# The opening of a two-layer attention and expert kernel written as one block

## The reference, cut to what matters

```python
def adaln_params(cvec, w, b):
    m = jax.nn.silu(cvec) @ w + b
    return [mi[..., None, :] for mi in jnp.split(m, ADA_CHUNKS, axis=-1)]

def modulate(x, g, shift, scale):
    return rmsnorm(x, g) * (1 + scale) + shift

        h = modulate(x, norm1_g[i], sh1, sc1)
        hc = modulate(xc, norm1_g[i], csh1, csc1)
```

## Time and profile before

| what | value |
|---|---|
| runs before, us | 4536.93, 4542.0, 4542.59 |
| median of the runs | 4542.0 us |
| span of the profiled execution | 4538.3 us |
| busy: PE / PEld / DVE / ACT / POOL | 80% / 58% / 49% / 35% / 4% |
| DMA, mean over the span | 200 GB/s, 909.64 MB |
| mean granted TensorE clock | 0.887 of full speed |

### The profile page before, as it was taken

One profiled execution on the slowest core, in us unless ns is written; L12 is line 12 of the kernel. 1 busy time (PEld: TensorE's weight loads), 2 busy tenths in 40 slices (PEclk: granted clock), 3 DMA queues, 4 the chain that ended last, 5 costly groups with the idle time before them and its releaser, 6 DMA issues. The chain is left out here.

```text
span 4538.3 us, 58330 instructions
## 1 busy us (share of the span) xinstructions
PE 3652.0 (80%) x19637; PEld 2640.8 (58%) x19637; DVE 2230.0 (49%) x4378; ACT 1566.0 (35%) x2639; POOL 168.9 (4%) x344
## 2 busy tenths in 40 slices
PE   5977977968699999998796689998368667777776
PEld 3747965447588888886565579997236322222223
DVE  3634643899566666665358778884441100000001
ACT  3433432128444444443241666663121111011111
POOL 0006610000000000000000000000000000000000
PEclk8988988979899999999897899999659788788878
DMA  4230021516644454443201499994212499999996
GB/s 161 73 132 13 13 96 52 210 45 199 217 175 182 185 185 175 168 173 126 98 20 65 126 362 312 312 312 140 116 38 84 189 428 427 427 427 428 427 428 273
DMA packets 331813, 909.64 MB, mean 200 GB/s; under 512 B 46592, under 2 KB 167168, under 8 KB 306176
## 3 DMA queue, kind: packets, MB, share of 16 engines
q1 hardware_dynamic: 331648, 907.42, 52.9%
HBM read 854.38 MB, written 52.95 MB: 200 GB/s over the span
## 5 line engine op out<-in xcount | busy, mean ns | idle before, releaser
L1929 PE MATMUL pd<-h_parts,u_parts 128*128 128x512 f32 x2048 | 471.3, 390 | 37.5 <-DVE u_parts L2015 37.5
L1942 PE MATMUL po<-act_parts,v_parts 128*128 128x512 f32 x2048 | 483.6, 393 | 10.3 <-DVE v_parts L2020 3.7
L1929 PEld LDWEIGHTS pd<-h_parts,u_parts 128*128 128x128 f32 x2048 | 385.6, 188 | 118.1 <-DVE u_parts L2015 37.7
L1942 PEld LDWEIGHTS po<-act_parts,v_parts 128*128 128x128 f32 x2048 | 383.6, 189 | 105.4 <-DVE v_parts L2020 22.4
L3053 PE MATMUL pb<-moe_ring,moe_xs 128*32 128x512 f32 x2048 | 334.4, 759 | 137.1 <-DMA moe_ring<-in_moe_gu 119.3
L3104 DVE TENSOR_TENSOR moe_hidden<-moe_silu,pg 128x512 f32<-128x512 f32 x16 | 11.0, 688 | 659.6 <-PE pg L3042 533.1
L2133 PE MATMUL pd<-h_parts,u_parts 128*128 128x256 f32 x2048 | 268.2, 284 | 38.6 <-DVE u_parts L2212 38.6
L2133 PEld LDWEIGHTS pd<-h_parts,u_parts 128*128 128x128 f32 x2048 | 264.6, 192 | 50.3 <-DVE u_parts L2212 39.2
L2143 PE MATMUL po<-v_parts,act_parts 128*128 128x512 f32 x1024 | 260.0, 398 | 0.9 <-DVE act_parts L2228 0.9
L395 PE MATMUL ps<-h_terms,w_terms 128*128 128x512 f32 x960 | 225.1, 398 | 40.6 <-DVE w_terms L408 40.6
L3069 PE MATMUL pd<-moe_ring,moe_hidden 128*32 128x512 f32 x1024 | 167.4, 790 | 100.6 <-DMA moe_ring<-in_moe_down 87.9
(11 more groups left out here) (472 smaller groups left out, 5846.8 us busy)
## 6 DMA issues: line engine op xcount, KB each, us to landing
moe_ring<-in_moe_gu SPq DMA_DIRECT2D x128, 2048.0 KB, 26.3
u_stream<-in_peer_u SPq DMA_DIRECT2D x256, 512.0 KB, 6.0
v_stream<-in_peer_v SPq DMA_DIRECT2D x256, 512.0 KB, 4.3
moe_ring<-in_moe_down SPq DMA_DIRECT2D x64, 2048.0 KB, 26.2
ada_ring<-in_ada_w SPq DMA_DIRECT2D x24, 2048.0 KB, 13.4
g_stream<-peer_gates SPq DMA_DIRECT2D x128, 256.0 KB, 5.9
peer_gates<-gate_stage_even SPq DMA_DIRECT2D x3, 8192.0 KB, 30.3
peer_gates<-gate_stage_odd SPq DMA_DIRECT2D x3, 8192.0 KB, 30.3
```

Source lines behind the costliest of these rows:

```text
L1929: m = pe.matmul(pd[:, j, 0:T], us[:, j, w, c], h[:, w, c], start=(c + w == 0), stop=(c == DC - 1 and w == 1))
L1942: m = pe.matmul(po[:, (c + b) % 4, 0:T], vs[:, j, w, (c + b) * P:(c + b) * P + P], aparts[:, 4 * half + j, w], start=(j + w == 0), stop=(j ...
```

## The change

`opening` takes the place of the first `load`, of `ada_params`, of the `load` of `deltas` and of `modulated` for layer 0. It is one block. SP issues `params`, `xT`, `consts`, the four modulation fetches, the two `w_qkv` fetches and `w_ab`, and `deltas`, one behind the other, and at the end waits for `deltas`. ACT does silu as soon as `params` is there and `c_silu` is cleared, then the squares when `xT` is there, the root, the four copies of the modulation, the shifts. PE does the sums first and then the modulation. DVE does eps, reciprocal, `place` (the addition of the bias), `mod_mult` and the 16 products, each of the first ones waiting for the one before through `Chain`. The ring's four slots are no longer a tile of their own: three are stretches of `qkvT` (8 chunks each) and one is `oT`. The silu and clear of `AdaParams` become methods, with their two blocks kept for the instances without a given ring; the `fetch` argument goes. The semaphores of the ring get names that the expert stream uses too.

```diff
--- before.py
+++ after.py
@@ -542,37 +542,40 @@
 
     TURN = 4
...
-    def __init__(self, k, ctx, layer, ada_w, params, consts, mod, fetch=True, first=0, groups=6 * D // BANK):
+    def __init__(self, k, ctx, layer, ada_w, params, consts, mod, first=0, groups=6 * D // BANK, ring=None):
-        self.slot = [k.sig(f"ada_slot{n}") for n in range(self.TURN)]
+        self.slot = [k.sig(f"ring_slot{n}") for n in range(self.TURN)]
-        self.ring = k.sb(ctx, "ada_ring", [self.TURN, DC, BANK])
+        if ring is None:
+            own = k.sb(ctx, "ada_ring", [self.TURN, DC, BANK])
+        self.ring = ring or [own[:, n] for n in range(self.TURN)]
-        with nc.Block() as block:
-            if fetch:
-                @block.sync
-                def _(sp):
-                    for g in range(self.TURN):
-                        self.fetch(sp, g)
-
-            @block.vector
-            def _(dve):
-                dve.memset(self.cs[:], 0.0)
-        with nc.Block() as block:
-            @block.scalar
-            def _(act):
-                act.activation(self.cs[:, :, 0:2], PARAMS(params, "cc").rearrange("p (c v) -> p c v", v=2), ACT.Silu)
+        if ring is None:
+            with nc.Block() as block:
+                @block.vector
+                def _(dve):
+                    self.clear(dve)
+            with nc.Block() as block:
+                @block.scalar
+                def _(act):
+                    self.squash(act)
+
+    def clear(self, dve):
+        return dve.memset(self.cs[:], 0.0)
+
+    def squash(self, act):
+        return act.activation(self.cs[:, :, 0:2], PARAMS(self.params, "cc").rearrange("p (c v) -> p c v", v=2), ACT.Silu)
-        sp.dma_start(self.ring[:, g % self.TURN], self.src[:, :, at:at + BANK]).then_inc(self.slot[g % self.TURN].h, DMA_DONE)
+        sp.dma_start(self.ring[g % self.TURN], self.src[:, :, at:at + BANK]).then_inc(self.slot[g % self.TURN].h, DMA_DONE)
...
@@ -607,43 +610,113 @@
...
+    def place(self, dve):
+        j0, n = 4 * self.first, 4 * self.GROUPS
+        a0 = PARAMS.at["ada_b"][0] + 48 * self.layer + j0
+        bias = self.params[:, a0:a0 + n].rearrange("p (j v) -> p j v", v=1).broadcast_to([P, n, 2])
+        return dve.tensor_tensor(self.mod[:, j0:j0 + n], self.pt[:, 0, 0:2 * n].rearrange("p (j v) -> p j v", v=2), bias, ALU.add)
+
+    def done(self):
+        for s in self.slot:
+            s.done(DMA_DONE * (self.GROUPS // self.TURN))
+        for s in (self.used, self.part_ready, self.turned):
+            s.done(self.GROUPS)
+
     def finish(self, k):
         with k.nc.Block() as block:
             @block.vector
             def _(dve):
-                j0, n = 4 * self.first, 4 * self.GROUPS
-                a0 = PARAMS.at["ada_b"][0] + 48 * self.layer + j0
-                bias = self.params[:, a0:a0 + n].rearrange("p (j v) -> p j v", v=1).broadcast_to([P, n, 2])
-                dve.tensor_tensor(self.mod[:, j0:j0 + n], self.pt[:, 0, 0:2 * n].rearrange("p (j v) -> p j v", v=2), bias, ALU.add)
-        for s in self.slot:
-            s.done(DMA_DONE * (self.GROUPS // self.TURN))
-        for s in (self.used, self.part_ready, self.turned):
-            s.done(self.GROUPS)
-
-
-def ada_params(k, layer, ada_w, params, consts, mod):
-
+                self.place(dve)
+        self.done()
+
+
+def opening(k, xT, hT, params, consts, deltas, mod, W, ring, begin):
+
+
+    nc = k.nc
+    one = CONSTS(consts, "one")
+    got_params, got_consts, got_x, got_deltas = (k.sig(x) for x in ("open_params", "open_consts", "open_x", "stage_loaded"))
+    sq, summed, rooted, chain, scaled = (k.sig(x) for x in ("nrm_sq", "nrm_sum", "nrm_root", "dve_chain", "nrm_scaled"))
+    spans = ((0, 0, CTX), (1, CTX, TALL))
+    CLEAR, RSTD, MOD, MULT = 1, 3, 4, 5
     with ExitStack() as ctx:
-        ada = AdaParams(k, ctx, layer, ada_w, params, consts, mod, groups=4)
-        with k.nc.Block() as block:
+        ada = AdaParams(k, ctx, 0, W["ada_w0"], params, consts, mod, groups=4, ring=ring)
+        mult = k.sb(ctx, "mod_mult", [2, DC])
+        x2 = k.sb(ctx, "x_squared", [DC, TALL])
+        rstd = k.sb(ctx, "rstd", [TALL])
+        ps = k.banks(ctx, 1)
+        with nc.Block() as block:
             @block.sync
             def _(sp):
-                ada.sync(sp)
+                sp.dma_start(params[:], W["params"]).then_inc(got_params.h, DMA_DONE)
+                sp.dma_start(xT[:], W["xT"]).then_inc(got_x.h, DMA_DONE)
+                sp.dma_start(consts[:], W["consts"]).then_inc(got_consts.h, DMA_DONE)
+                ada.begin(sp)
+                for x in begin:
+                    x.begin(sp)
+                sp.dma_start(deltas[:], W["deltas"]).then_inc(got_deltas.h, DMA_DONE)
+                sp.wait_ge(got_deltas.h, got_deltas.at(DMA_DONE))
+
+            @block.scalar
+            def _(act):
+                act.wait_ge(got_params.h, got_params.at(DMA_DONE))
+                act.wait_ge(chain.h, chain.at(CLEAR))
+                ada.squash(act).then_inc(rooted.h, 1)
+                act.wait_ge(got_x.h, got_x.at(DMA_DONE))
+                for c in range(DC):
+                    act.activation(x2[:, c, :], xT[:, c, :], ACT.Square).then_inc(sq.h, 1)
+                act.wait_ge(chain.h, chain.at(RSTD - 1))
+                act.activation(rstd[:], rstd[:], ACT.Sqrt).then_inc(rooted.h, 1)
+                for g in range(ada.GROUPS):
+                    ada.scalar(act, g)
+                m = 0
+                for c in range(DC):
+                    for v, a, b in spans:
+                        m += 1
+                        act.wait_ge(scaled.h, scaled.at(m))
+                        act.activation(hT[:, c, a:b], hT[:, c, a:b], ACT.Identity, bias=mod[:, c:c + 1, v])
 
             @block.tensor
             def _(pe):
+                pe.wait_ge(got_consts.h, got_consts.at(DMA_DONE))
+                for c in range(DC):
+                    pe.wait_ge(sq.h, sq.at(c + 1))
+                    mm = pe.matmul(ps[:, 0, :], one, x2[:, c, :], start=(c == 0), stop=(c == DC - 1))
+                mm.then_inc(summed.h, 1)
+                pe.wait_ge(rooted.h, rooted.at(1))
                 for g in range(ada.GROUPS):
                     ada.tensor(pe, g)
                     if g:
                         ada.turn(pe, g - 1)
                 ada.turn(pe, ada.GROUPS - 1)
 
-            @block.scalar
-            def _(act):
-                for g in range(ada.GROUPS):
-                    ada.scalar(act, g)
-        ada.finish(k)
-
+            @block.vector
+            def _(dve):
+                link = Chain(dve, chain)
+                link(ada.clear(dve))
+                dve.wait_ge(summed.h, summed.at(1))
+                link(dve.tensor_scalar(rstd[:], ps[:, 0, :], 1.0 / D, EPS, ALU.mult, ALU.add))
+                dve.wait_ge(rooted.h, rooted.at(2))
+                link(dve.reciprocal(rstd[:], rstd[:]))
+                dve.wait_ge(ada.turned.h, ada.turned.at(ada.GROUPS))
+                link(ada.place(dve))
+                a0 = PARAMS.at["norm1_g"][0]
+                for v in range(2):
+                    m = dve.scalar_tensor_tensor(out=mult[:, v], in0=mod[:, DC:2 * DC, v], scalar=1.0, in1=params[:, a0:a0 + DC],
+                                                 op0=ALU.add, op1=ALU.mult)
+                link(m)
+                for c in range(DC):
+                    for v, a, b in spans:
+                        dve.scalar_tensor_tensor(out=hT[:, c, a:b], in0=xT[:, c, a:b], scalar=mult[:, v, c:c + 1],
+                                                 in1=rstd[:, a:b], op0=ALU.mult, op1=ALU.mult).then_inc(scaled.h, 1)
+        ada.done()
+    for s in (got_params, got_consts, got_x, got_deltas):
+        s.done(DMA_DONE)
+    sq.done(DC)
+    summed.done(1)
+    rooted.done(2)
+    chain.done(MULT)
+    scaled.done(2 * DC)
 
 
 def gdn_qkv(k, parts, params, qkvT, raw, stream):
...
+                    opening(k, xT, hT, params, consts, deltas, mod, W, [qkvT[:, 8 * n:8 * n + 8] for n in range(3)] + [oT[:]], (w_qkv, w_ab))
                     raw = k.sb(c3, "qkv_raw", [2, 2, SEQ + 4])
                     parts = k.sb(c3, "h_terms", [2, DC, TALL], F32R)
                     split_terms(k, hT, DC, parts)
                     gdn_qkv(k, parts, params, qkvT, raw, w_qkv)
-                ada = AdaParams(k, c2, 0, W["ada_w0"], params, consts, mod, fetch=False, first=4, groups=8)
+                ada = AdaParams(k, c2, 0, W["ada_w0"], params, consts, mod, first=4, groups=8)
                 linear_tok(k, hT, DC, 4, ab, w_ab, (ada,))
                 normalise_heads(k, qkvT[:, 0:16], 16, TALL, consts, 1.0, lambda h: float(P) ** -0.5 if h < 8 else 1.0, ada=ada)
                 ada.finish(k)
@@ -3162,15 +3235,12 @@
         xT = k.sb(ctx, "xT", [DC, TALL])
         x2 = xT[:, :, CTX:TALL]
         C = lambda name: CONSTS(consts, name)
-        load(k, [(consts[:], W["consts"]), (params[:], W["params"]), (xT[:], W["xT"])])
```

(10 more changed lines are left out.)

## The result

The changed kernel takes 4512.97 us (median of four runs, 4512.73 to 4516.06), the kernel before 4541.89 (four runs): ratio 0.994, 95% interval 0.9927 to 0.9953. That is 28.9 us less, where 24.0 were forecast, and 4513.0 where 4518.0 was. The profiled execution took 4513.02 with a span of 4511.1, against 4538.3 before. A second series gave 25.8 us less (4513.33 against 4539.09), so the size of the gain is known to some 3 us from the times, and better from the timeline.

The account below looks back on a forecast made before the run. The opening's row of hardly overlapping steps was taken as the bound, ending at 71.25 us. Fetch at 32.5 plus tail 14.8 gives 47.3, saving 23.95: 4542.0 - 24.0 = 4518.0 us, range 4511.5 to 4527.5.

Parts of the forecast that it names:

- The path: Opening, first 71 us: load, modulation and norm run in a row; the change takes 23.95 us off, ending compute at 47.3.
- the norm's leg: Opening: squares, sums, root and reciprocal finish by 27, under the fetches, zero on the path; uncovered it would cost 15 us.
- Order in the queue: Opening's transfers: served in order at 387 GB/s, fourth modulation fetch landing at 32.5 (31.8 to 33.3), `deltas` at 44.7 to 46.2.
- The tail behind the last fetch: Opening, after the fourth modulation fetch: 7.25 us to the bias at low clock, 14.8 to the last addition.
- A: Opening's end: compute ends the block, last modulation group at low clock; 4518 us, chance 0.55.
- rival B: Opening's end: clock stays high or the fetch is early, `deltas` ends the block at 45 to 46.5; 4516.5 us, chance 0.25.
- Nothing behind the opening moves: Projection and everything later: shifts as a whole with the opening's end, its length unchanged.
- the distance between median and span: Whole run: the median stands 3.7 us above the profiled span, unaltered by the change, so span 4514.3 gives 4518.0.
- C: Opening, PE: low clock from sums to end, compute over at 56.2, gain 15 us; 4527 us, chance 0.08.
- D: Opening's queue: transfers served side by side, modulation landing at about 45, gain 11.4 us; 4530.6 us, chance 0.04.
- E: Behind the opening: nothing is won because a later part waits for something that doesn't move; 4542 us, chance 0.05.
- F: Opening's queue: rate collapses with eleven transfers queued, block ends at 83.6, 12.4 us late; 4554 us, chance 0.03.

Follow-up runs that it names:

- early_deltas_later: early_transfers with the issue of `deltas` moved from the modulation's block to the norm's block; 4530.95 us (one run).
- early_transfers: Changed kernel with the opening's work back in the separate blocks of before, transfers still issued early; 4538.73 us, ratio 0.9996 to before, second series 0.9987.
- qkv_first: Changed kernel with the two `w_qkv` fetches and `w_ab` issued ahead of the four modulation fetches; 4529.21 us, ratio 0.9974 to before.
- later_deltas: Changed kernel with the wait for `deltas` moved out of the opening to the block clearing the state ahead of the delta rule; 4514.93 us, ratio 0.9948.
- warm_products: later_deltas plus two filler products on PE ahead of each of modulation groups 2 and 3; 4516.17 us, ratio 0.9950 to before.
- scale_first_warm: later_deltas with scale fetched and used before shift, plus one filler PE product before the third modulation group, two before the fourth; 4510.48 us, ratio 0.9943.

## Why the prediction was right, point by point

- *The path.* Load, modulation, norm in a row, and the norm's leg hidden under the fetches: as forecast. The splits of 71.52, 60.89, 59.92 and 46.36 divide the 25.2 us into 10.6 for earlier transfers (with `deltas` off the path), 1.0 for merged blocks and 13.6 for the overlap of the norm. The merged blocks' share is the least certain: the clock moves each split by about 1 us, and 0.4 of the 1.0 is the empty block behind the norm, which only early_deltas_later has. The leg that I priced at 15 us is worth 13.6. This division is of the opening; in the times, early_transfers was 1.0 us slower and in the second series 6.1 faster than before, with openings 7.5 and 8.4 shorter, for a reason that stays open.
- *Order in the queue, 387 GB/s over eleven transfers.* Held (31.79, and qkv_first). I took 32.5 between 31.8 and 33.3; the lower end came. `xT` landed at 8.9, where the sum at full rate gives 9.0 for it now that it stands ahead of `consts`, and not at 11.6: later transfers seem to fill its uneven end, as the stretches from 4 to 12 have 382 GB/s or more. The 358 GB/s of the Trainium skill (DMA: Bandwidth & Descriptors, section Bandwidth) didn't come: the stretches of 2 us from 12 to 40 have 384 to 389. The same section gives 358 for two cores of one memory streaming at once, and its single-core measurements reach 425; here one core ran.
- *The norm's leg.* Forecast until 27, measured 24.3, with 7.5 us to spare before the last fetch.
- *The tail behind the last fetch, the mis-sized term.* 7.25 to the bias was taken from the one row of before; it measured 5.38 and 5.57 in the changed kernel, 6.58 in later_deltas, 7.25 in qkv_first, 3.91 in warm_products. The last group was at low clock, as A says, but the clock rose before the turns (1.95, not 3.58). Compute ended at 44.7, and not at 47.3: 0.7 of that is the fetch and 1.9 the tail. So four signs that I had named missed on the early side: the last group (31.79, not 32 to 33.5), the bias (37.17, not 39 to 41), the last addition (44.69, not 46 to 48.5) and the projection's first product (55.08, not 56 to 57).
- *The block's end.* With compute early, `deltas` decided, at 45.9, inside the 44.7 to 46.2 forecast for it. So it was rival B, priced at 4516.5, and not the likeliest case A, which ended the opening. It came with the sign that I had listed against A, SP waiting when ACT was done. Of B's two reasons the early fetch held in full and the high clock only for the turns. The number suffers little from naming the wrong one only because A and B are priced 1.5 us apart.
- *Nothing behind the opening moves.* Within the scatter it held: rest 4458.0 and 4456.8 before, 4456.0 and 4457.1 in the changed kernel. The 2.0 us more in the profiled spans aren't shown to be an effect of the change.
- *The sum against 4513.0.* The forecast was 5.0 too long: 1.2 in the opening (24.0 against 25.2), 2.0 in the rest, 1.7 from the distance between median and span, and 0.1 from a fourth run of before. The distance was the weakest term: "nothing in the change alters what lies around the span" is right for the 1.7 to 2.0 that nearly every run shows, but the rest of my 3.7 was the luck of one profiled execution. All these errors point the same way; the time is 1.5 above the range's lower end of 4511.5.
- *Rivals C, D, E and F.* C falls, as the clock was high at 26.36 and 36; D by qkv_first. F falls by the stretches, and its premise never came up: from the third fetch on SP was held at each issue. The six fetches landed at 15.4, 20.9, 26.3, 31.7, 37.1 and 43.9, so at most four of them were out at a time, as before, and `deltas` was issued only at 33.81. What eleven transfers at once would do isn't shown. E doesn't hold for this change, but early_transfers is close to it: 7.5 us less in the opening and a ratio of 0.9996, then 8.4 less and 0.9987.

## What to carry to other kernels

Where blocks stand in a row and each waits for its own transfers, write down for each transfer when it could land if all were issued at the start, and find the last one that compute needs; everything not depending on it belongs ahead of it. Then look at what else the block waits for: here a transfer that nothing needed until much later was the last to land, and everybody waited for it. A later split of that one dependency (scale before shift) took another 4 to 5 us off the opening.

An issue isn't free when much is still in front of it in the queue. It holds the issuing engine, and through the end of the block all the others (2.76 us in early_transfers).

## What I had not expected of the hardware

- Issuing 640 KB took 0.34 us with an empty queue, 0.56 with about 1.5 MB in front (early_deltas_later), the first 2 MB fetch of the modulation 0.43 with 2.7 MB in front, and the 640 KB again 5.3 to 6.2 us where, as an estimate from the 387 GB/s, some 3.2 to 3.6 MB of fetches were still in front (5.29 in qkv_first, with about 5.3 MB). The bytes of the transfer itself don't set it: `w_ab`, 128 KB, took 7.50 us to issue in the changed kernel (26.3 to 33.8), longer than any of the 2 MB fetches there.
- The clock doesn't follow from the idle time ahead of a piece of work alone. The third group ran at high clock after 2.49 us of idle time in the changed kernel (1.92), and at the low one after 1.93 in later_deltas (3.26) and after 0.66 in scale_first_warm (3.35), with nearly the same work on PE before it. In scale_first_warm the granted clock was still 1.00 in the stretch 26 to 27 and 0.55 in 27 to 28, so it fell inside the group, while PE was busy.
- The 4.46 ms behind the opening vary by up to 12 us between profiles of kernels that have the same instructions there, which is more than many of the effects studied here. Only the timeline of the opening can tell those apart.
